# An encoder layer in fp32 on one core: constants loaded by SyncE, the first row of x in chunks, weight splits and reciprocals moved at stage borders, forget gates one unit earlier

## The reference, cut to what matters

```python
def trunk_layer(x, pe, mixer, ffn1, mix_g, merge_w, ffn2, ple):
    x = x + 0.5 * swiglu_ffn(x, *ffn1)
    h = rms_norm(x, mix_g)
    o_a, o_b, state = mixer(h)
    x = x + merge_branches(h, o_a, o_b, *merge_w)
    x = x + 0.5 * swiglu_ffn(x, *ffn2)
    x = x + per_layer_embedding(x, pe, *ple)
    return x, state

def swiglu_ffn(x, g, w_in, w_out):
    h = rms_norm(x, g)
    gate, up = jnp.split(h @ w_in, 2, axis=-1)
    return (jax.nn.silu(gate) * up) @ w_out

def project_heads(h, w_in, b_f, qn_a, kn_a, qn_b, kn_b):
    qa, ka, va, qb, kb, vb, fl = jnp.split(h @ w_in, pts, axis=-1)
    ...
    logf = jax.nn.log_sigmoid(fl.astype(jnp.float32) + b_f.astype(jnp.float32))
```

## Time and profile before

| | |
|---|---|
| median of 3 runs | 2634.94 us (2632.8 to 2637.18) |
| the profiled execution | 2638.77 us, of it 2637.1 us in the span of the trace |
| PE busy | 2601.9 us, 99% of the span |
| DVE, ACT, POOL busy | 51%, 27%, 4% |
| mean granted clock of PE | 0.994 |
| bytes moved | 140.09 MB, mean 53 GB/s |

### The profile page before, as it was taken

One profiled execution on the slowest core, in us unless ns is written; L12 is line 12 of the kernel. 1 busy time (PEld: TensorE's weight loads), 2 busy tenths in 40 slices (PEclk: granted clock), 3 DMA queues, 4 the chain that ended last, 5 costly groups with the idle time before them and its releaser, 6 DMA issues.

```text
span 2637.1 us, 39357 instructions
## 1 busy us (share of the span) xinstructions
PE 2601.9 (99%) x15684; PEld 2450.6 (93%) x15684; DVE 1335.8 (51%) x2581; ACT 722.6 (27%) x1398; POOL 115.7 (4%) x156
## 2 busy tenths in 40 slices
PE   9999999999999899999999999999999999999999
PEld 9999999999998788777779989899999999999999
DVE  6444444444457675555433434554454444445664
ACT  5111111111124576555421111421111111111331
POOL 0000000000003000111100000300000000000210
PEclk9999999999999999999999999999999999999999
DMA  4111111111113211221131111111111111111112
GB/s 149 43 44 45 43 47 42 48 41 49 41 49 127 64 37 33 67 71 45 43 108 41 43 45 42 40 41 42 48 41 48 41 48 41 49 41 48 57 41 92
DMA packets 41677, 140.09 MB, mean 53 GB/s; under 512 B 5728, under 2 KB 8200, under 8 KB 41376
## 3 DMA queue, kind: packets, MB, share of 16 engines
q1 hardware_dynamic: 40944, 137.23, 16.5%
q10 hardware_dynamic: 560, 0.28, 0.0%
HBM read 122.91 MB, written 16.15 MB: 53 GB/s over the span
## 4 chain that ended last, share of the span: by engine, by line
PE 94%; DVE 3%; ACT 2%; issue 0%; ACTq 0%; DVEq 0%
PE psum L518 73%; PE psum L658 9%; PE psum L819 5%; PE psum L731 2%; PE psum L688 2%; PE psum L707 2%; PE psum L749 1%; ACT h_hi L864 1%; DVE w_lo L483 1%; ACT square L875 1%; DVE x L1177 0%; ACT w_hi L478 0%; DVE rstd L1129 0%; DVE ple_gate L1450 0%; ACT probs L976 0%
## 5 line engine op out<-in xcount | busy, mean ns | idle before, releaser
L518 PE MATMUL psum<-h_hi,w_hi 128*128 128x364 f32 (+1 forms) x2688 | 889.6, 331 | 14.6 <-DVE x L1177 10.7
L518 PE MATMUL psum<-h_hi,w_lo 128*128 128x364 f32 (+1 forms) x2688 | 885.7, 330 | 0.1
L518 PE MATMUL psum<-h_lo,w_hi 128*128 128x364 f32 (+1 forms) x2688 | 885.6, 329 | 0.0
L518 PEld LDWEIGHTS psum<-h_hi,w_hi 128*128 128x128 f32 x2688 | 507.4, 189 | 21.7 <-issue 10.2
L518 PEld LDWEIGHTS psum<-h_lo,w_hi 128*128 128x128 f32 x2688 | 507.1, 189 | 1.2
L518 PEld LDWEIGHTS psum<-h_hi,w_lo 128*128 128x128 f32 x2688 | 507.3, 189 | 0.0
L518 PE MATMUL psum<-hid_hi,w_hi 128*128 128x364 f32 x1296 | 425.9, 329 | 3.2 <-DVE hid_lo L1144 3.2
L518 PE MATMUL psum<-hid_lo,w_hi 128*128 128x364 f32 x1296 | 424.9, 328 | 0.0
L518 PE MATMUL psum<-hid_hi,w_lo 128*128 128x364 f32 x1296 | 424.5, 328 | 0.0
L1177 DVE SCALAR_TENSOR_TENSOR x<-psum,x 128x364 f32<-128x364 f32 (+1 forms) x624 | 318.8, 531 | 173.8 <-PE psum L518 173.4
L1138 DVE TENSOR_TENSOR pre<-psum,rstd 128x364 f32<-128x364 f32 x153 | 81.5, 535 | 393.0 <-PE psum L518 391.6
(11 more groups left out here) (137 smaller groups left out, 2127.4 us busy)
## 6 DMA issues: line engine op xcount, KB each, us to landing
w_raw<-w_units SPq DMA_DIRECT2D x193, 512.0 KB, 3.6
x<-x_t SPq DMA_DIRECT2D x8, 544.0 KB, 9.3
x_saved<-x SPq DMA_DIRECT2D x8, 544.0 KB, 5.4
x<-x_saved SPq DMA_DIRECT2D x8, 544.0 KB, 8.5
y_out<-x SPq DMA_DIRECT2D x8, 544.0 KB, 3.9
f_keys<-f_cumulative SPq DMA_DIRECT2D x4, 1024.0 KB, 6.4
f_samp<-f_cumulative SPq DMA_DIRECT2D x4, 576.0 KB, 7.1
kb_out<-k SPq DMA_DIRECT2D x4, 544.0 KB, 3.1
```

The source lines that it names most:

```text
L518: mm = pe.matmul(out, w[:, slot, w_cols], m, start=first and n == 0, stop=last and n == 2)
```

## The change

Five edits. (1) The five transfers of constants are issued by SP, behind the loads of x, three of them behind unit 2, and no longer by ACT. (2) Row 0 of x is split in three chunks on ACT and DVE, and PE waits by chunk in block 0. (3) At borders ACT splits ahead of n = 10 and 16 (`FINAL_HI`) and DVE ahead of 12 and 19. (4) The three reciprocals stand ahead of the three reads in all four stages (norms 0 to 3). (5) In the mixer the unit of the forget gates stands ahead of the first query unit, `log_forget` moves from slots 6 and 7 to slots 3 and 4, and the turned values of the first value unit are spread between the head sums.

```diff
-FINAL_SPLITS = {0: 1, 12: 2, 18: 3}
+FINAL_SPLITS = {0: 1, 12: 2, 19: 3}
+FINAL_HI = {0: 1, 10: 2, 16: 3}
-MIX_UNITS = [("ka", 0, 1), ("va", 0, 2), ("qa", 0, 3), ("f", 0, 0), ("qa", 1, 4), ("qa", 2, 5), ("kb", 0, 8),
+MIX_UNITS = [("ka", 0, 1), ("va", 0, 2), ("f", 0, 0), ("qa", 0, 3), ("qa", 1, 4), ("qa", 2, 5), ("kb", 0, 8),
...
+    first_q = UNIT_OF["qa", 0]
     for n, (kind, pair, _) in enumerate(MIX_UNITS):
+        if n == first_q:
+            values(1, 0, 0)
         if n >= 2 and kind[0] in "qk":
             for c in range(NCH):
                 sums(n, c, CHUNK_END[NCH * (n - 2) + c] + 1)
+                if n == first_q and c:
+                    values(1, c, 0)
...
-                    pe.wait_ge(h_lo_done, 24 * norm + NCH * (k + 1))
+                    if norm or k:
+                        pe.wait_ge(h_lo_done, 24 * norm + NCH * (k + 1))
...
+                            if norm == k == j == 0:
+                                pe.wait_ge(h_lo_done, c + 1)
...
-                    if slot == DENSE:
+                    if slot == NCH:
                         log_forget()
...
-            act.dma_start(onehot[:], constants[0:N_BUCKETS, 3 * P:3 * P + REL]).then_inc(consts_in, 16)
-            act.dma_start(table[:], rel_table).then_inc(consts_in, 16)
-            act.dma_start(consts[:], constants[:, 0:3 * P]).then_inc(consts_in, 16)
-            act.dma_start(head_gain[:], head_gains).then_inc(consts_in, 16)
-            act.dma_start(b_f[:], b_forget).then_inc(consts_in, 16)
...
+                    if norm is not None and tile == 0:
+                        for c in range(NCH):
+                            inverse(norm, c)
                     for c, (c0, n) in enumerate(CH):
-                        if norm is not None and tile == 0:
-                            inverse(norm, c)
                         read_scaled(pre[:, c0:c0 + n], et + c, c, norm if tile == 0 else None)
...
-                    if slot == DENSE + 1:
+                    if slot == NCH + 1:
                         log_forget()
...
             for m in range(1, KD):
                 load_x(m)
+            sp.dma_start(onehot[:], constants[0:N_BUCKETS, 3 * P:3 * P + REL]).then_inc(consts_in, 16)
+            sp.dma_start(table[:], rel_table).then_inc(consts_in, 16)
             load_unit(sp, At(2))
+            sp.dma_start(consts[:], constants[:, 0:3 * P]).then_inc(consts_in, 16)
+            sp.dma_start(head_gain[:], head_gains).then_inc(consts_in, 16)
+            sp.dma_start(b_f[:], b_forget).then_inc(consts_in, 16)
```

More of the change, by code:

```diff
@@ L173, in stat_table, with values @@
         sums(0, c, 0)
+    def values(v, group, ready):
+        use(ready, ("values", len(turned), v, group))
+        turned.append((v, group))
+    first_q = UNIT_OF["qa", 0]
     for n, (kind, pair, _) in enumerate(MIX_UNITS):
+        if n == first_q:
+            values(1, 0, 0)
         if n >= 2 and kind[0] in "qk":
@@ L177, in stat_table @@
                 sums(n, c, CHUNK_END[NCH * (n - 2) + c] + 1)
-        if kind[0] == "v" and n >= 2 or n == 2:
-            v = 1 if n == 2 else n
+                if n == first_q and c:
+                    values(1, c, 0)
+        if kind[0] == "v" and n >= 2:
             for group in range(3):
-                use(0 if n == 2 else UNIT_END[n] + 1, ("values", len(turned), v, group))
-                turned.append((v, group))
+                values(n, group, UNIT_END[n] + 1)
     return uses, normed, turned
@@ L908, in ffn @@
                 for n in range(24):
-                    if n in FINAL_SPLITS:
-                        k = FINAL_SPLITS[n]
+                    if n in FINAL_HI:
+                        k = FINAL_HI[n]
                         split_hi(act, u + k, s + k)
@@ L1033, in _ @@
                 act.wait_ge(x_in[m], 16)
-                act.activation(h_hi[:, m, :], x[:, m, :], ACT.Copy, scale=gain[:, m:m + 1]).then_inc(h_hi_done, NCH)
+                for c0, w in CH if m == 0 else [(0, TOK)]:
+                    act.activation(h_hi[:, m, c0:c0 + w], x[:, m, c0:c0 + w], ACT.Copy,
+                                   scale=gain[:, m:m + 1]).then_inc(h_hi_done, NCH if m else 1)
                 if m == 0:
@@ L1326, in mix @@
             def mix(e):
+                for c in range(NCH):
+                    inverse(1, c)
                 for c, (c0, n) in enumerate(CH):
-                    inverse(1, c)
                     read_scaled(k0[:, c0:c0 + n], e + c, c, 1)
@@ L1347, in mix @@
                         read_chunk(x)
-                    if slot == DENSE - 1:
-                        dve.wait_ge(pr_free, 2 * NCH)
+                    if slot == NCH - 1:
+                        dve.wait_ge(pr_free, NCH)
                         dve.tensor_scalar(f_pre[:], f_pre[:], b_f[:, 0:1], None, ALU.add).then_inc(f_step, 2)
-                    if slot == DENSE + 1:
+                    if slot == NCH + 1:
                         log_forget()
@@ L1357, in _ @@
             for m in range(KD):
-                dve.wait_ge(h_hi_done, NCH * (m + 1))
-                dve.scalar_tensor_tensor(h_lo[:, m, :], x[:, m, :], gain[:, m:m + 1], h_hi[:, m, :].bitcast(F32),
-                                         ALU.mult, ALU.subtract).then_inc(h_lo_done, NCH)
+                for c, (c0, w) in enumerate(CH if m == 0 else [(0, TOK)]):
+                    dve.wait_ge(h_hi_done, NCH * (m + 1) if m else c + 1)
+                    dve.scalar_tensor_tensor(h_lo[:, m, c0:c0 + w], x[:, m, c0:c0 + w], gain[:, m:m + 1],
+                                             h_hi[:, m, c0:c0 + w].bitcast(F32), ALU.mult,
+                                             ALU.subtract).then_inc(h_lo_done, NCH if m else 1)
                 if m == 0:
@@ L1433, in _ @@
                         split_lo(dve, u + 1, s + 1)
+                    if half == m == 0:
+                        for c in range(NCH):
+                            inverse(3, c)
                     for c, (c0, n) in enumerate(CH):
-                        if half == m == 0:
-                            inverse(3, c)
                         read_scaled(ple_gate[:, m, c0:c0 + n], e + c, c, 3 if half == m == 0 else None)
```

4 lines of the change are left out of this document (2 added, 2 removed).

## The result

| | before | after |
|---|---|---|
| median of 17 runs each, same chip | 2634.21 us (2632.62 to 2637.18) | 2640.49 us (2637.57 to 2642.93) |
| ratio after/before, 95% interval | | 1.0023 (1.0016 to 1.0029) |
| profiled execution, its clock | 2638.77 us, 0.994 | 2639.14 us, 0.996 |

The change costs 6.3 us by the medians, 6.1 by the ratio. The two profiled executions differ by 0.4 only: the one of before that I worked from took 1.6 longer than the longest of the 17 timed runs (2637.18). The experiments show what that did to the sum.

What follows compares the result with a forecast made beforehand. PE, busy 99% of the span, bounds the kernel, so only its waits and lower clock count. Terms 2.3 + 1.5 + 3.3 + 1.5 - 9.3 - 3.9 - 1.2 + 2.8 = -3.0 gave 2631.9 us by the median, range 2626 to 2639.

Steps and rivals of the forecast that it cites:

- constants and norm 0: Start: late constants +2.3 and low stretch +1.5; three reciprocals ahead of the first read +3.3 and low stretch +1.5.
- row 0: Start: chunks shorten the first wait of 1.78, but ahead of the wait for constants, so worth nothing.
- splits, three borders: Three borders: earlier splits remove the wait and its low stretch, leaving 1.1 of small waits; -3.1 each, -9.3 in all.
- reciprocals, norms 1 to 3: Mixer: wait for k goes with its low stretch, -3.9; norm 2: 0; PLE: w_lo's wait goes, -1.2.
- (a): Mixer: PE's wait of 2.0 for DVE's k, forecast to go with its low stretch and 0.4 around it, -3.9.
- forget gates: Mixer: new waits of 2.1, 4.9 and 3, 10.0 in place of 7.3; low stretches stay two; +2.8 (-1 to +5).
- low stretch: After some PE waits, matmuls run at 1.2 GHz instead of 2.4; priced at 1.5 us each.
- The step that failed: Throughout the sum: a low stretch follows waits of 1.7 to 3.5, none follow a wait near 1.
- (c): Mixer: PE's wait of 2.1 for neg_top, said to come of DVE's 5.7 us for the forget gates.
- Rivals: Constants not late, 0.08; borders heal fully and gates' third wait hidden, 0.17; borders not healing, 0.12; as summed, 0.63.
- Rival 3: Borders: no healing, since DVE's pushed adds cost PE about 2 and keep the low stretch; +6.3, 2641.2; chance 0.12.

Runs made afterwards that it cites:

- e1: The kernel before, unchanged, timed and profiled once more: median 2634.27 us, 0.9999 of before; its profiled execution took 2634.11.
- e7: Changed kernel with constants back on ACT and reciprocals and reads taking turns in norm 0, forget gates still first: 2630.21 us, 0.9986 of before.
- e10: Kernel before with only row 0 of x split in three chunks: 2632.23 us, 0.9995 of before.
- e5: Kernel before with only the border splits moved (ACT ahead of 10 and 16, DVE of 12 and 19): 2628.01 us, 0.9982 of before.
- e6: Kernel before with only the reciprocals put together ahead of the reads at norms 1 to 3: 2630.67 us, 0.9990 of before.
- e4: Changed kernel with constants on ACT, norm 0 mixed again, and the forget-gate edit undone, turned values included: 2624.67 us, 0.9960 of before.
- e9: Changed kernel, constants still on SP, but PE waits ahead of block 2 only for onehot and table: 2635.79 us, 1.0002 of before.
- e11: Changed kernel with all five constants on SP, issued ahead of rows 1 to 7 of x: 2632.93 us, 0.9998 of before.

## Why the prediction was wrong

I predicted 2631.9 (a sum of -3.0) with a range up to 2639, and measured 2640.49, +6.1 by the ratio. Each thing that was to show a step right did: PE stood ahead of the table matmul until 19.29 (18.5 to 20), waited for `pre`, had no first wait and no 0.50 stretch at the border and no wait for k, and waited 2.3, 4.8 and 3.0 in the mixer (2, 5 and 3). The mechanisms were right, and the sizes of the terms were not. "In the traces" sets the changed kernel against e1, by the start times of the same matmul ahead of the place and behind it:

| term | predicted | by the runs | in the traces | what differs |
|---|---|---|---|---|
| constants and norm 0 | +8.6 | +9.8 (e7) | +9.6, with row 0 | low time |
| row 0 | 0 | -1.3 (e10) | above | within the interval |
| splits, three borders | -9.3 | -4.7 (e5) | -5.5 | price of low time |
| reciprocals, norms 1 to 3 | -5.1 | -2.6 (e6) | -3.5 | low time behind (a) |
| forget gates | +2.8 | +6.8 (e7 to e4) | +5.5 | low time |
| sum | -3.0 | +8.0, the whole +6.1 | +6.1 | |

The two traces as a whole are 4.9 apart: e1 has a low stretch at the end of the mixer that the changed kernel's execution happens not to have (-1.7), and they drift by 0.5 elsewhere.

**The step that failed** is "In the sum I let a low stretch follow a wait of the size of those that had one", with the price of 1.5 for each, in three ways. At the borders (-4.5 of the -9.3) the stretches were real and did go, at 10 of 12 borders against none of 30, but each cost 0.67 to 1.04 where small waits follow it, and e5's whole saving was 1.62 to 2.30 a border, not 3.1. Behind (a) (-1.5 of the -3.9) the stretch was chance: only the profile that I predicted from has it. And the gates' "low stretches stay at two" is wrong: e1 has one there, the kernels with the gates in the old place one or two, and the changed kernel three. The waits alone were well priced: a border 1.6 predicted (2.3 + 0.4 - 1.1) and 1.62 measured, the waits for k and w_lo 3.6 predicted and 3.5 in e6's trace. The execution that I took the stretches from had more of them than any of e1's (0.994 against 0.996 and 0.997). I saw that its time lay 3.8 above the median and subtracted that at the end, but then spent the same stretches again as savings.

**The added waits** went the other way. The five new waits of 2.3 to 4.8 were priced at the same 1.5, with as many stretches as before in the mixer. 3.83 for the constants was followed by two stretches, and the table matmul itself took 1.44 in place of 0.81. The whole can be checked once more from the other side. The list of waits of e1 has 11 rows that sum to 32.5, that after sums to 36.5, so 4.0. The mean clock over the changed kernel's 17 executions is 0.9954, over e1's 0.9965, and 0.0011 is 1.7 us at the measured 1.5 for each 0.001. Together 5.7, against 6.1 measured. The clock's part is rough, as executions of before beside other experiments have means from 0.9958 to 0.9963.

**Constants.** Right in kind (late by their place in SP's queue; e9 and e11). Of the two rules of the Trainium skill in "DMA: Bandwidth & Descriptors" the one on rings and order is the one that these runs bear out; "Issuing engines are not separate DMA queues" would have made the move free. Late by 3.3 where 2.3 was summed: the last landed about 0.4 later than 18.9, and the table matmuls ran at half clock.

**Forget gates.** The three waits were predicted at 10.0 in all and came to 10.1. What they replaced was summed as 7.3, and is 6.3 in e4, where wait (c) came to 1.1 in place of 2.1. With the third low stretch that I had kept for the upper end of +5, the term ended at 6.8 by the ratios and 6.1 in the traces of e7 and e4.

**Rivals.** None came true by itself. Rival 3's time (2641.2) came near for another reason: its mechanism, borders that do not heal, did not happen, since DVE's pushed adds cost 0.88 and not 2. The match is luck.

## What to carry to other kernels

Before a wait is priced, profile the unchanged kernel more than once. What all profiles show (here the waits at borders and in the mixer, to 0.05) is the kernel's, what some show (here the low-clock stretches behind them) is to be weighed by how often it comes and by what it costs at that place, not added at full price. A short transfer that the bottleneck needs early belongs ahead of the long ones in its queue, or behind a wait of its own; whichever engine issues it. And before a block of work on an in-order engine is moved forward, look for what it now pushes toward its deadline: cutting it into pieces helped where the chain had slack, and not where the move had used it up.

## What the runs showed of the hardware that I had not expected

- Two executions of one kernel with the same waits differ in their low-clock stretches: at the first border and behind (a) the profile of before was at 0.50 and e1 at 1.00, while at the second and third border both were at 0.50. At the end of the mixer, in unchanged code, there were two, one or none.
- A low stretch is cheaper than its matmuls say where small waits follow it: 1.04 and 0.67 at borders, in place of 1.5. At the end of the mixer, from 24.90 in e1 to 23.22 in e6, it cost 1.68.
- With no low stretch between 25 and 811 in either, e1 started block 2 0.06 earlier than the profile of before and left the border's wait 0.96 later. What makes this drift of 1.0 us in 790 was not tried, and it sets a floor to what two traces can tell.
